# The up projection's 1056 tokens as 512, 512 and 32 columns per matrix product, for three times 352

## What is computed

```
x = x + concat([o, y_sc]) @ w_out
u_ff = relu(rmsnorm(x, norm_mlp) @ w_up)
x = x + (u_ff * u_ff) @ w_down
gate = sigmoid(rmsnorm(x, norm_ple) @ w_ple_gate)
x = x + gate * (p @ w_ple_proj)
```

## Time and profile before

| | |
|---|---|
| median of 3 runs | 1676.21 us (1675.53 to 1676.34) |
| span of the profiled execution, first to last instruction | 1676.7 us |
| mean granted TensorE clock | 0.974 of full |
| PE busy | 1605.3 us, 96%, 10169 products |
| weight loads busy | 1548.0 us, 92% |
| DVE busy | 718.7 us, 43% |
| ACT busy | 540.9 us, 32% |
| POOL busy | 301.0 us, 18% |
| DMA | 86.64 MB, 52 GB/s in the mean |

### The profile page before, as it was taken

One profiled execution on the slowest core, in us unless ns is written; L12 is line 12 of the kernel. 1 busy time (PEld: TensorE's weight loads), 2 busy tenths in 40 slices (PEclk: granted clock), 3 DMA queues, 4 the chain that ended last, 5 costly groups with the idle time before them and its releaser, 6 DMA issues.

```text
span 1676.7 us, 27623 instructions
## 1 busy us (share of the span) xinstructions
PE 1605.3 (96%) x10169; PEld 1548.0 (92%) x10169; DVE 718.7 (43%) x1190; ACT 540.9 (32%) x865; POOL 301.0 (18%) x361
## 2 busy tenths in 40 slices
PE   6999999999999966999999999999999999999997
PEld 6999899898998955898999999999999999998997
DVE  5566534444454436224433333333333333335435
ACT  6233423425244243226330312112121303126335
POOL 5100151533525223221000000000000000032113
PEclk9999999999999967899999999999999999999998
DMA  6111010201003030521111111111111111111202
GB/s 159 39 50 50 25 39 14 63 13 51 13 13 128 0 108 5 154 79 47 51 38 51 44 45 51 43 46 50 38 51 50 38 50 39 50 50 34 69 26 104
DMA packets 135717, 86.64 MB, mean 52 GB/s; under 512 B 16507, under 2 KB 130843, under 8 KB 135654
## 3 DMA queue, kind: packets, MB, share of 16 engines
q1 hardware_dynamic: 134502, 81.48, 16.7%
q0 software_dynamic: 1152, 4.33, 0.6%
HBM read 74.58 MB, written 11.21 MB: 51 GB/s over the span
## 4 chain that ended last, share of the span: by engine, by line
PE 76%; issue 9%; DVE 6%; POOL 4%; ACT 3%; DMA 1%; SPq 1%; POOLq 0%; DVEq 0%; ACTq 0%
PE pg L547 63%; PE bk L690 3%; PE bk L699 3%; PE pg L648 2%; PE bk L697 2%; DVE act_lo L1605 1%; ACT act_hi L955 1%; POOL Tb L1871 1%; PE bk L853 1%; POOL qg L1881 1%; DMA ysc_spill<-cv 1%; DVE cv L1451 1%; POOL XT L1884 1%; PE bk L936 1%; POOL XT L1886 1%
## 5 line engine op out<-in xcount | busy, mean ns | idle before, releaser
L547 PE MATMUL pg<-act_hi,w_hi 128*128 128x352 f32 x1464 | 479.9, 328 | 11.3 <-issue 4.8
L547 PE MATMUL pg<-act_lo,w_hi 128*128 128x352 f32 x1464 | 473.2, 323 | 0.0
L547 PE MATMUL pg<-act_hi,w_lo 128*128 128x352 f32 x1464 | 473.0, 323 | 0.0
L547 PEld LDWEIGHTS pg<-act_hi,w_hi 128*128 128x128 f32 x1464 | 278.1, 190 | 15.9 <-issue 9.9
L547 PEld LDWEIGHTS pg<-act_lo,w_hi 128*128 128x128 f32 x1464 | 278.4, 190 | 0.0
L547 PEld LDWEIGHTS pg<-act_hi,w_lo 128*128 128x128 f32 x1464 | 277.7, 190 | 0.0
L547 PE MATMUL pg<-u_hi,w_hi 128*128 128x352 f32 x768 | 249.3, 325 | 0.0
L547 PE MATMUL pg<-u_hi,w_lo 128*128 128x352 f32 x768 | 248.9, 324 | 0.0
L547 PE MATMUL pg<-u_lo,w_hi 128*128 128x352 f32 x768 | 247.8, 323 | 0.0
L1940 POOL TENSOR_TENSOR ssq<-ssq,sq 128x352 f32<-128x352 f32 x72 | 77.8, 1094 | 892.2 <-ACT sq L955 891.3
L955 ACT ACTIVATE w_hi<-w_raw 128x1024 fp32r<-128x1024 f32 x111 | 116.7, 1052 | 302.2 <-PE pg L547 285.1
(11 more groups left out here) (290 smaller groups left out, 1961.2 us busy)
## 6 DMA issues: line engine op xcount, KB each, us to landing
w_raw<-in_w_up SPq DMA_DIRECT2D x32, 512.0 KB, 4.0
w_raw<-in_w_down SPq DMA_DIRECT2D x32, 512.0 KB, 3.4
w_raw<-in_w_in SPq DMA_DIRECT2D x29, 512.0 KB, 3.9
x_tok<-in_x_prompt SPq DMA_DIRECT2D x8, 512.0 KB, 7.8
w_raw<-in_w_out SPq DMA_DIRECT2D x8, 512.0 KB, 4.8
x_col<-in_x_prompt SPq DMA_DIRECT2D x8, 512.0 KB, 3.6
w_raw<-in_w_ple_gate SPq DMA_DIRECT2D x8, 512.0 KB, 3.8
out<-y_tok SPq DMA_DIRECT2D x8, 512.0 KB, 3.1
```

Source lines behind the costliest of these rows:

```text
L547: last = mm(pg[bank][:, 0:TH], w, a, start=i == 0, stop=i == len(terms) - 1)
```

## The change

Up units alone get a procedure of their own, `wide_unit`, and a division of their own, `wide_cols`: 512, 512 and 32 columns. It sends the same 72 products per unit with the same weights in the same order, and signals the same counts. DVE's and ACT's steps of the up units take the same ranges; `tm` and `sq` grow to 512 columns. As the input's split and `r_b` are still made by thirds of 352, up unit 0 waits for two thirds of the split before its first group and for all before the others, and DVE waits for all of `r_b` before each of its reads in chunk 0. Down units and everything else keep their thirds. No engine's order of instructions changes.

```diff
+WT = 512
...
+        def wide_cols(n):
+            return slice(n * WT, min((n + 1) * WT, T))
...
-        tm = [sb(f"tm{i}", [P, TH], scope=tail) for i in range(2)]
-        sq = [sb(f"sq{i}", [P, TH], scope=tail) for i in range(2)]
+        tm = [sb(f"tm{i}", [P, WT], scope=tail) for i in range(2)]
+        sq = [sb(f"sq{i}", [P, WT], scope=tail) for i in range(2)]
...
+            def wide_unit(b, p, ready, then=None):
+
+                panel_ready(b, p)
+                slot = b % 2
+                for n in range(3):
+                    pe.wait_ge(*ready(n))
+                    pe.wait_ge(sm.evacuated, twelfths(b, p, 4 * n - 8))
+                    w = wide_cols(n).stop - wide_cols(n).start
+                    for k in range(KD):
+                        mm(pg[n][:, 0:w], w_hi[slot][:, k, :], act_hi[:, k, wide_cols(n)], start=k == 0, stop=False)
+                        mm(pg[n][:, 0:w], w_hi[slot][:, k, :], act_lo[:, k, wide_cols(n)], start=False, stop=False)
+                        last = mm(pg[n][:, 0:w], w_lo[slot][:, k, :], act_hi[:, k, wide_cols(n)],
+                                  start=False, stop=k == KD - 1)
+                    last.then_inc(sm.mm_done, 4)
+                    if then is not None and n == 1:
+                        then()
...
-                            unit(u + x, i, KD, act_hi, act_lo, lambda n: (sm.split_lo, KD * (n + 1)),
-                                 then=mlp_sums if i == x == 0 else None)
+                            wide_unit(u + x, i, lambda n: (sm.split_lo, KD * min(n + 2, 3)),
+                                      then=mlp_sums if i == x == 0 else None)
...
-                            unit(u + x, i, KD, act_hi, act_lo, lambda n: (sm.split_lo, KD * (n + 1)))
+                            wide_unit(u + x, i, lambda n: (sm.split_lo, 3 * KD))
...
-                                    dve.wait_ge(sm.rms_ready, n + 1)
+                                    dve.wait_ge(sm.rms_ready, 3)
+                                w = wide_cols(n).stop - wide_cols(n).start
...
-                                stt(tm[g % 2][:, :], pg[n][:, 0:TH], 0.0, r_b[:, cols(n)], MAX, MUL) \
+                                stt(tm[g % 2][:, 0:w], pg[n][:, 0:w], 0.0, r_b[:, wide_cols(n)], MAX, MUL) \
...
-                                tt(rows(u_lo[c % 2][:, k, cols(n)]), sq[g % 2][:, :],
-                                   rows(u_hi[c % 2][:, k, cols(n)]).bitcast(f32), SUB).then_inc(sm.u_lo_made, 1)
+                                tt(rows(u_lo[c % 2][:, k, wide_cols(n)]), sq[g % 2][:, 0:w],
+                                   rows(u_hi[c % 2][:, k, wide_cols(n)]).bitcast(f32), SUB).then_inc(sm.u_lo_made, 1)
```

More of the change, by code:

```diff
@@ L1191, in out_pair @@
                             op(token[:, 16 + n:17 + n], token[:, 13:14], ACT.Copy)
-                        op(sq[g % 2][:, :], x_flat[:, ds(i * 2 * T + x * T + n * TH, TH)], ACT.Square) \
+                        op(sq[g % 2][:, 0:TH], x_flat[:, ds(i * 2 * T + x * T + n * TH, TH)], ACT.Square) \
                             .then_inc(sm.sq_made, 1)
@@ L1215, in _ @@
                                 act.wait_ge(sm.u_lo_made, at(base, i, 6))
-                                op(sq[g % 2][:, :], tm[g % 2][:, :], ACT.Square).then_inc(sm.usq_made, 1)
+                                w = wide_cols(n).stop - wide_cols(n).start
+                                op(sq[g % 2][:, 0:w], tm[g % 2][:, 0:w], ACT.Square).then_inc(sm.usq_made, 1)
                                 act.wait_ge(sm.usq_made, at(2 + base, i, 6))
@@ L1220, in _ @@
                                 act.wait_ge(sm.consts_made, 3)
-                                op(u_hi[c % 2][:, ds(2 * i + x, 1), cols(n)].rearrange("p a t -> p (a t)"),
-                                   sq[g % 2][:, :], ACT.Copy).then_inc(sm.u_hi_made, 1)
+                                op(u_hi[c % 2][:, ds(2 * i + x, 1), wide_cols(n)].rearrange("p a t -> p (a t)"),
+                                   sq[g % 2][:, 0:w], ACT.Copy).then_inc(sm.u_hi_made, 1)
                             unit_done(u + x, i)
@@ L1234, in _ @@
                                 act.wait_ge(sm.ssq_added, at(3 * KD + 6 * x + g + 1, i, 12))
-                                op(sq[g % 2][:, :], xres[:, 4 * i + 2 * x + g // 3, cols(g % 3)], ACT.Square) \
+                                op(sq[g % 2][:, 0:TH], xres[:, 4 * i + 2 * x + g // 3, cols(g % 3)], ACT.Square) \
                                     .then_inc(sm.sq_made, 1)
@@ L1278, in gates @@
                             op(gate[:, ds(2 * i + x, 1), cols(n)].rearrange("p a t -> p (a t)"),
-                               tm[(3 * x + n) % 2][:, :], ACT.Sigmoid).then_inc(sm.gate_made, 1)
+                               tm[(3 * x + n) % 2][:, 0:TH], ACT.Sigmoid).then_inc(sm.gate_made, 1)
                             if (hf, i, x, n) == (0, 1, 1, 1):
@@ L1290, in _ @@
                     act.wait_ge(sm.ssq_added, 6 * KD + 12 * hf + g + 1)
-                    op(sq[g % 2][:, :], xres[:, k, cols(n)], ACT.Square).then_inc(sm.sq_made, 1)
+                    op(sq[g % 2][:, 0:TH], xres[:, k, cols(n)], ACT.Square).then_inc(sm.sq_made, 1)
                     act.wait_ge(sm.sq_made, 6 * KD + 12 * hf + g + 1)
@@ L1700, in gates @@
                             dve.wait_ge(sm.gate_made, at(12 * hf + g + 1, i, 6))
-                            tt(tm[g % 2][:, :], pg[n][:, 0:TH], r_b[:, cols(n)], MUL).then_inc(sm.evacuated, 4)
+                            tt(tm[g % 2][:, 0:TH], pg[n][:, 0:TH], r_b[:, cols(n)], MUL).then_inc(sm.evacuated, 4)
                             if (hf, i, x, n) == (0, 1, 1, 1):
@@ L1711, in _ @@
                     product_ready(u + 4, 0, g + 1)
-                    tt(tm[g % 2][:, :], pg[g % 3][:, 0:TH], gate[:, d, cols(n)], MUL).then_inc(sm.evacuated, 1)
+                    tt(tm[g % 2][:, 0:TH], pg[g % 3][:, 0:TH], gate[:, d, cols(n)], MUL).then_inc(sm.evacuated, 1)
                     dve.wait_ge(sm.evacuated, twelfths(u + 4, 0, g + 1))
                     x_t = xres[:, 4 * hf + d, cols(n)]
-                    tt(x_t, x_t, tm[g % 2][:, :], ADD).then_inc(sm.x_made, 1)
+                    tt(x_t, x_t, tm[g % 2][:, 0:TH], ADD).then_inc(sm.x_made, 1)
                     if (hf, g) == (1, 9):
@@ L1939, in add_squares @@
                 pool.wait_ge(sm.sq_made, at(base + g + 1, i, step))
-                tt(ssq[:, cols(n)], ssq[:, cols(n)], sq[g % 2][:, :], ADD).then_inc(sm.ssq_added, 1)
+                tt(ssq[:, cols(n)], ssq[:, cols(n)], sq[g % 2][:, 0:TH], ADD).then_inc(sm.ssq_added, 1)
             pool.wait_ge(sm.sample_states_out, 16 * H)
```

## The result

| | before | changed |
|---|---|---|
| median of 4 runs each | 1676.28 us (1675.53 to 1680.19) | 1768.79 us (1767.69 to 1773.88) |
| span of the profiled execution | 1676.7 us | 1767.8 us |
| mean granted TensorE clock | 0.974 | 0.967 |

The changed kernel takes 1.0542 times as long (95% interval 1.0527 to 1.0556), 92.5 us more; the forecast was 1765.5 us.

A forecast was written before the change was run, and what follows sets the result against it. TensorE was taken as the bound: number of products times spacing of their starts. Products 66.9, start 6.2 and clock 16 make 89 us on the profiled 1676.7, 1766, or 1765.5 us as median; 8-in-10 range 1722 to 1806 us.

The forecast's parts named there:

- The long products: Up units' 512-column products: a fixed 13.4 ns over the columns, 226.7 ns each, bounds 216.6 and 232.9.
- The short products: Up units' 32-column products: each bound by its 128 x 128 weight load, 114 ns; bounds 62 and 160.
- The sum: All up units: two long and one short product replace three of 352, 87.1 ns more, 768 times: +66.9 us.
- The start: First up unit: later waits for split, sums and `r_b` delay unit two to 803.2: +6.2 us beyond the products.
- The clock: Short groups in up units: ten of 32 stretches bring a fall to half clock, 1.6 us each: +16 us.
- Nothing: Evacuation, DVE and ACT work, banks and weight arrival in up units: covered by products, no added time.
- that loads hide and the change gains: Rival, up units: weights pulled ahead, short products 27 ns, long 216.6, total 1667 us; chance 3%.
- Loads as fast as a transpose's: Rival, up units' short products at 62 ns: +27.0 us and 6.2, total 1710 us; chance 8%.
- The floor of 160 ns per load and product: Rival, up units' short products at 160 ns: +102 us and 6, 1785 us, up to 1836 with clock; chance 7%.
- A clock that holds: Rival, up units: no falls, 66.9 + 6.2, total 1750 us; inside the forecast's own range, no separate chance.
- one that falls in every unit: Rival, all up units: 73 + 51, total 1801 us; inside the forecast's own range, no separate chance.
- The rule of the Trainium skill: Product spacing in up units: columns / 2.4 + 2.5 ns, floor about 25 ns; 456.6 per triple, so a gain.

The follow-up runs named there:

- e3: Changed kernel with its tokens divided as 512, 272 and 272 columns: 1694.09 us, 1.0087 of the kernel before.
- e8: Changed kernel with its tokens divided as 480, 480 and 96 columns: 1743.46 us, 1.0392 of the kernel before.
- e11: Changed kernel with its tokens divided as 416, 320 and 320 columns: 1689.97 us, 1.0067 of the kernel before.
- e7: Changed kernel with 22 of each group's 24 up products using 64 of 128 weight columns: 1728.50 us, 1.0302 of the kernel before.
- e5: Changed kernel with the 32-column products placed between the second group's long ones, three and three per depth block: 1781.32 us, 1.0620 of the kernel before.
- e2: Kernel before, thirds of 352 kept, with only the changed kernel's late waits in chunk 0: 1685.51 us, 1.0042 of the kernel before.
- e6: Changed kernel with each group of 32 columns computed twice, 48 products for 24: 1928.54 us, 1.1492 of the kernel before.
- e1: Changed kernel with chunk 0 back in thirds of 352 with the old waits, chunks 1 to 7 unchanged: 1751.41 us, 1.0426 of the kernel before.
- e4: Changed kernel with 3 products in place of 24 in each up unit's 32-column group: 1705.78 us, 1.0164 of the kernel before.

## Why the prediction came out

The mechanism held: the short products are bound by their loads, the start comes later, and the clock falls now and then. That 1765.5 us came within 3.3 of the measured 1768.8 is in part luck, as the errors of the terms cancel: the products were 8 us too small and the clock 7 too large. All terms in order:

1. *The long products* were mis-sized. I took a fixed 13.4 ns over the columns, 226.7 ns, and kept 232.9 as the upper bound; measured are 232.2. The 13.4 ns are not fixed (e3, e8, e11). So a wider product gains nothing on a column: 0.4535 ns at 512, 0.452 at 352. The lower bound of 216.6 rested on one spacing of two float32 products that the rows give to 10 ns, too coarse for an excess of 3.
2. *The short products*: 114 ns taken, 111.8 measured. That they cost a load each is shown from three sides: by e8 (96 columns at the same price), e7 (half a load, half the price) and e5 (no place hides them).
3. *The sum* was 66.9 us and is 75.1: a triple (two long products and a short one, for three of 352 columns) costs 97.8 ns more (9.39 us over 96 triples) where I had 87.1. By the spacings it is 2 x 5.5 for the long ones, less 2.2 for the short one, and 3 x 1.1 since thirds in steady units ran at 159.0, not at 160.1: 12 ns, of which the blocks show 11.
4. *The start*: 6.2 us forecast, 5.7 measured in the account, with unit two at 805.83 where I had 803.2: 2.0 us of the difference are the half clock that the longer stop brings, which I had not placed there (the second group started at 793.11, with the split done at 791.0), 0.7 come from ahead of the MLP and 0.1 from unit 0's own products; `r_b` and the evacuation took 0.2 less than I had. e2 shows this cost alone: 6.8 us with its clock.
5. *The clock* was over-sized: 16 us for ten falls, against 9 us for five stretches, only two of them in steady units and a third behind the stop at 850. The mechanism stands: e6, with the stretches of short products twice as long, lost some 74 us to it, and e5, without any such stretch, had none in steady units. The same step of the forecast ("ten falls, a third") had no row to fix the count, and e1's runs, 8 us apart, suggest that there is no fixed count.
6. *Nothing* was right for the changed kernel, where no steady unit waits; but the reading behind it was off. Behind a second group stand not 5.4 us of long products but 2.7 of short ones, and a bank is not free a whole unit ahead: down units start on the evacuation of the last up unit's second group. In e4 and e5, where the short group is gone from the unit's end, that shows as 0.7 us a block.

The rivals: that loads hide and the change gains is refuted by e5 and e7. Loads as fast as a transpose's did not come; the 62 ns of the earlier trace rows hold for transposes. The floor of 160 ns per load and product is refuted by 111.8. A clock that holds (1750 us) was 19 us off, one that falls in every unit (1801) 32. One figure is a slip: the change would gain below a short product of 39.0 ns, not 38.5 (480.3 - 433.2 - 8.1); nothing hangs on it.

The rule of the Trainium skill, "TensorE: Matmul & The Clock Gate", section on the back-to-back issue gap, against which I had set the trace, would have had 215.8 and 25 ns; the trace disagrees with both, at 232.2 and 111.8. I had left out that the section calls this the gap of single products and gives some 131 ns at 512 columns for a stream of loads and products, which is what this kernel has; the trace's 232.2 ns disagree with that too.

No version that computes all tokens beats the kernel before. The time of 1056 columns is nearly the same for every division tried whose parts are of 272 columns or more (45.8 to 46.4 us a block, thirds the least); narrower parts pay the difference to a load. By 111.8 / 0.452 that limit is at some 250 columns, an estimate, as nothing between 96 and 272 was run.

## What to carry to other kernels

When every product loads its own weights, count per product the larger of two times, its columns' and its load's, and divide evenly: a full bank gains nothing, and a remainder of 32 columns costs as much as one of 96 (in 28 units: 8 us inside thirds, 75 us alone). Before moving a remainder, ask also what now waits for the whole where it waited for a part, and what the remainder's time was covering. A busy PE says nothing about its clock: look at the grant wherever products are short.

## What was not expected of the hardware

- A float32r product costs 0.452 to 0.461 ns per column from 272 to 512 columns, while at half clock 352 columns took 292.7 ns, 0.83 ns a column, with nothing over. Plain float32 products of 512 columns, spaced 0.43 us, fill two cycles a column at 2.4 GHz (0.427) to within the rounding of the rows. Halving the load beside a float32r product takes off 1.7 ns (e7). What makes the rest is open: it wasn't tried with other operands or with DVE and ACT idle.
- Down units' products of 352 columns take 161.8 ns in both kernels, up units' of the same width 159.0; this was not looked into.
- The number of half-clock stretches seems to differ between runs of one program (e1: 1745.49 to 1753.78 us, mean granted clock 0.976 to 0.968).
